# The low parts of the mixers' weights, made in quarters in every slot instead of halves in two slots of four

## The chip, the core and the metric

The program runs on one core of one Trainium2 chip. The core has a matrix engine (TensorE, PE in the profile), a vector engine (VectorE, DVE), an engine for activation functions (ScalarE, ACT), a general one (GpSimd, POOL) and an engine that here only starts DMA transfers (SyncE, SP). Each runs its own list of instructions in order; they meet at semaphores. SBUF is the on-chip memory with 128 partitions, PSUM the memory that PE writes. The metric is the device time of one execution in microseconds, lower is better.

## The reference, cut to what matters

The program is a first block (rotary attention beside an mLSTM, then a gated feed-forward net), then two layers, each a feed-forward net, a mixer and a second feed-forward net, over 256 tokens of width 1024, all in float32:

```python
for i in range(DEPTH_2):                                   # DEPTH_2 = 2
    h = rmsnorm(x, ffn1_norm[i])
    x = x + 0.5 * swiglu(h, ffn1_w_gate[i], ffn1_w_up[i], ffn1_w_down[i])
    h = rmsnorm(x, mix_norm[i])
    proj = h @ w_in[i]                                     # 1024 x 2560: q_s, k_s, v_s, q_m
    mkv = rmsnorm(mem, mem_norm[i]) @ w_mem_kv[i]          # 1024 x 512
    o_m = memory_attention(q_m, k_m, v_m)
    # layer 0: chunked_rel_attention; layer 1: rotary q and k, diff_attention
    x = x + jnp.concatenate([o_s, o_m], axis=-1) @ w_out[i]   # 1024 x 1024
    ...
```

## The kernel before, in words

**Products in three parts.** Every float32 product is made of three rounded ones: with `a = a_hi + a_lo` and `w = w_hi + w_lo`, PE adds `a_hi·w_hi`, `a_hi·w_lo` and `a_lo·w_hi` (function `three`, L1461 to L1463 in the profile). So each weight has to be split before PE can use it.

**Units.** The weights stream through SBUF in units of 128 partitions x 2048 elements (1 MB). A unit takes four steps: SP fetches it into `raw[:, c % 3]` (L326), ACT copies it, rounded, into `whi[:, c % 3]` and increments `hi_done`, DVE subtracts (`wlo = raw - whi`) and increments `lo_done`, PE uses it and increments `unit_used`. Each of the three buffers exists three times. SP may fetch unit c + 3 only when `lo_done` says that unit c has been split; ACT may write `whi` for unit c + 3 only when PE has used unit c.

**A mixer is 60 slots.** In the two mixers (L = 0 and 1) PE, ACT and DVE each run a Python loop `for h in range(SLOTS)` over slots h = 0 to 59, unrolled. In slots 0 to 47 PE makes a quarter of a unit's products (`dense(h)`: six matmuls of 512 columns), in slots 48 to 59 a quarter of an output unit (`out_part(h)`). So PE begins unit n of the mixer (c = u + n, u = MEMU[L]) in slot 4n, and waits there for its `lo_done`:

```python
if h % 4 == 0:
    pe.wait_ge(lo_done, c + 1)
```

Between these products PE puts the attention: scores of item j in slot S_AT[j] (25, 27, 29, 31, 33, 35, 37, 39, 43, 44, 46 to 51), the turn of its probabilities two slots later, the product with the values three slots later. ACT rounds unit n in slots 4n-8 and 4n-7 (a half in each), and does exponentials and copies. DVE, in each of its slots, does in this order: `heads_rest` (L1355), `head_sum` (L896), in layer 1 `differential_norm` (L1402), `head_scale` (L1374), `y_rest` (L1363), `scores` (L987 and L989, or L1002), in layer 1 the rotation of queries and keys (L957, L962, L965; `rotated`), then the low part of a unit (`lo_half`, L1345), then in layer 1 `combine` (L1016 to L1020), then `group_out` (L1390, L1392). Each engine's list is fixed; an engine may be some slots behind another as long as the semaphores allow.

**The low parts in the mixers.** DVE makes the halves of unit n in its slots 4n-6 and 4n-5, and nothing of this kind in 4n-4 and 4n-3. The unit after the mixer's last one (the first of the next feed-forward net) is split in slots 58 and 59.

After the loop `boundary` adds PE's last sums to the residual rows (`residual`, L939) and prepares the next net's input.

Of the kernel before, what the change touches and what calls it, by code (L numbers as in the profile page):

```python
# [44 lines left out]
FFU = [30, 63, 112, 145, 194]  # L45
# [93 lines left out]
def build(nc, t, out):  # L139
# [7 lines left out]
    with ExitStack() as ctx:  # L147
# [702 lines left out]
        def _(dve):  # L850
# [8 lines left out]
            def lo(u, c0=0):  # L859

                dve.wait_ge(hi_done, u + 1)
                v = slice(c0, UW)
                dve.tensor_tensor(wlo[:, u % 3, v], raw[:, u % 3, v], whi[:, u % 3, v], ALU.subtract)\  # L863
                    .then_inc(lo_done, 1)
# [39 lines left out]
            def turned_gain(T, n, parts):  # L904
                for b in parts:
                    dve.wait_ge(xhi_done, 4 * T + b + 1)
                    bank = TURN_BANKS.get(T, range(4))[b]
                    for c in (2 * b, 2 * b + 1):
                        ins = dve.scalar_tensor_tensor(out=xlo[:, c, :], in0=ps[:, bank, SEQ * (c % 2):SEQ * (c % 2) + SEQ],  # L909
                                                       scalar=gain_col(n, c), in1=xhi[:, c, :],  # L910
                                                       op0=ALU.mult, op1=ALU.subtract)
                    ins.then_inc(xlo_done, 1)

            def boundary(T, n, idx, u_last, f, u, banks=(4, 6)):

                if f is not None:
                    dve.wait_ge(frs_ready, FRS_READY[f])
                scale = [1.0 if f is None else frs[:, r:r + 1] for r in range(RT)]
                residual(idx, u_last, scale[0], 0, banks)
                residual(idx, u_last, scale[1], 1, banks, (0,))  # L920
                turned_gain(T, n, (0, 1))
                residual(idx, u_last, scale[1], 1, banks, (1,))
                turned_gain(T, n, (2, 3))
                lo(u + 1)
                if n == N_F1:
                    dve.wait_ge(tr_ps, 4 * T + 4)
                    for r in range(RT):
                        scaled(N_FIN, res, res, r)
                lo(u + 2)

            def residual(idx, u_last, factor, r, banks=(4, 6), parts=range(2)):

                for h in parts:
                    if (r, h) < (1, 1):
                        dve.wait_ge(acc_ready, 3 * idx + 2 * r + h + 1)
                    else:
                        dve.wait_ge(unit_used, u_last + 1)
                    v = slice(512 * h, 512 * h + 512)
                    dve.scalar_tensor_tensor(out=res[:, r, v], in0=ps[:, banks[r] + h, :], scalar=factor,  # L939
                                             in1=res[:, r, v], op0=ALU.mult, op1=ALU.add).then_inc(res_done, 1)  # L940
# [156 lines left out]
            for r in range(RT):  # L1097
                for h in range(2):
                    v = slice(512 * h, 512 * h + 512)
# [236 lines left out]
            for L in range(2):  # L1336
                ffn(1 + 2 * L, FFU[1 + 2 * L], 2)
                u, e0, i0, base = MEMU[L], E0[L], IT0[L], STREAM0 + 12 * L
                T, n, idx, f = T_M0 + 3 * L, N_M0 + 3 * L, R_F1 + 3 * L, 1 + 2 * L

                def lo_half(c, part):

                    dve.wait_ge(hi_done, c + 1)
                    v = slice(1024 * part, 1024 * part + 1024)
                    ins = dve.tensor_tensor(wlo[:, c % 3, v], raw[:, c % 3, v], whi[:, c % 3, v], ALU.subtract)  # L1345
                    if part:
                        ins.then_inc(lo_done, 1)

                def heads_rest(h):
# [32 lines left out]
                def group_out(g):  # L1382

                    i, c = i0 + 4 * g, 16 + 8 * (g % 2)
                    heads, size = (2, 2 * HD) if ITEMS[i][0] == "D" else (4, HD)
                    total = sums[:, 2 * i:2 * i + 8]
                    if heads == 2:
                        total = total.rearrange("p (j e) -> p j e", e=2)[:, :, 0]
                    dve.wait_ge(p_ready, SOFT[i + 3])
                    link(dve.reciprocal(rec[:, c:c + 2 * heads], total))  # L1390
                    dve.wait_ge(pv_ready, i + 4)
                    dve.tensor_tensor(xn[:, :, 256 * g:256 * g + 256].rearrange("p r (h d) -> p r h d", d=size),  # L1392
                                      ps[:, 1, :].rearrange("p (r h d) -> p r h d", r=RT, d=size),
                                      rec[:, c:c + 2 * heads].rearrange("p (r h) -> p r h", r=RT).unsqueeze(3)
                                      .to_broadcast([P, RT, heads, size]), ALU.mult).then_inc(o_copied, 1)
# [19 lines left out]
                for h in range(SLOTS):  # L1415
                    if h in (4, 8):
                        turned_gain(T, n, (h // 2 - 2, h // 2 - 1))
                    if L == 0 and h == S_AT[0]:
                        dve.wait_ge(toep_ready, 1)
                    if h - 1 in HEAD_TURNS:  # L1420
                        heads_rest(h - 1)
                    if 0 <= h - 1 < 40 and (h - 1) % 8 in (5, 7):
                        k = 2 * ((h - 1) // 8) + ((h - 1) % 8 == 7)
                        head_sum(e0 + tile_event(L, k), MH if k // 2 in (0, 2) else 8, HD)
                    if L == 1:
                        for g in (0, 2, 3):
                            if h == V_AT[4 * g + 3] + 2:
                                head_sum(e0 + SUB_EVENT[g], 4, 2 * HD)
                            if h == V_AT[4 * g + 3] + 3:
                                differential_norm(g)  # L1430
                    for r, d in enumerate((9, 10)):
                        if h >= d and (h - d) % 8 == 0 and (h - d) // 8 in (0, 1, 3, 4):
                            head_scale(2 * ((h - d) // 8) + r)
                    if h - 1 in Y_TURNS[L]:
                        y_rest(Y_TURNS[L][h - 1])
                    if h in S_AT:
                        scores(i0 + S_AT.index(h))
                    if L == 1 and (h - 1) // 8 in (1, 3, 4) and (h - 1) % 8 in (5, 7):
                        rotated(2 * ((h - 1) // 8) + ((h - 1) % 8 == 7))
                    if h >= 2 and (h + 6) % 4 < 2:  # L1440
                        lo_half(u + (h + 6) // 4, (h + 6) % 4)
                    if L == 1 and h in S_AT:
                        combine(i0 + S_AT.index(h))
                    if h in V_AT and V_AT.index(h) % 4 == 3:
                        group_out(V_AT.index(h) // 4)
                boundary(T_F2 + 3 * L, N_F2 + 3 * L, R_WO1 + 3 * L, WO[1 + L] + 3, None, FFU[2 + 2 * L])
                if L == 0:
                    ffn(2, FFU[2], 2)
# [562 lines left out]
```

## Time and profile before

| | |
|---|---|
| median of 3 runs | 1406.43 us |
| lowest and highest | 1405.89 and 1407.33 us |
| the profiled execution, its own time | 1406.34 us |
| its span, first to last instruction | 1404.5 us |
| around the span | 1.84 us |
| first mixer, from its first low part in slots to its end | 585.5 to 711.0 us of the span |
| second mixer, the same stretch | 1082.5 to 1208.5 us of the span |
| granted clock of TensorE | 1.00 in the mixers (0.998 over the span) |

The profile is of one execution. Times in a row are microseconds from the start of the span. An instruction's duration overlaps with its follower's by a little (on DVE) or by much (matmuls on PE: 0.39 us long, one started every 0.23 us), so what a row costs its engine is read from the distance of two starts.

### The profile page before, as it was taken

Reading aid. Unit: us, or ns where it says so; the run is one execution under the profiler, and the core shown is the slowest. Engines: PE = TensorE matmul, PEld = TensorE weight load, DVE = VectorE, ACT = ScalarE, POOL = GpSimd, SP = SyncE. Lnnn points to the kernel's source line nnn. Section 1 sums busy time; section 2 is a strip of 40 time slices with the busy share of each in tenths; the row PEclk is TensorE's granted clock in tenths of the full one; section 3 lists DMA queues with packets and bytes.
Section 4 is the critical chain, followed back from the end, with each engine's and each line's share of the span. In section 5 each row is a group of like instructions: output and inputs, shape, how many; then the busy total and the mean of one; then the engine's idle time right before and its main releaser. Section 6 shows DMA issues by size and latency. Waiting matters only on the chain.

```text
span 1404.5 us, 19169 instructions
## 1 busy us (share of the span) xinstructions
PE 1375.3 (98%) x7393; PEld 1166.7 (83%) x7393; DVE 939.6 (67%) x1158; ACT 710.5 (51%) x921; POOL 128.1 (9%) x145
## 2 busy tenths in 40 slices
PE   6999999999999999999999999999999989999998
PEld 5888888888888888888888888888888867788887
DVE  4975676766677666765567666666667778666665
ACT  4656436444464444576654444544445666554442
POOL 3000003000030000032020000100000321300000
PEclk9999999999999999999999999999999999999999
DMA  9444456756546555553355565465665442466561
GB/s 269 155 156 145 150 180 243 236 188 199 181 143 215 183 192 194 164 189 109 109 173 187 181 195 192 135 224 181 192 196 180 155 146 91 143 196 200 181 198 70
DMA packets 165451, 246.33 MB, mean 175 GB/s; under 512 B 5800, under 2 KB 122708, under 8 KB 165264
## 3 DMA queue, kind: packets, MB, share of 16 engines
q1 hardware_dynamic: 161952, 240.14, 52.8%
q0 software_dynamic: 1776, 4.74, 1.2%
q8 instruction: 38, 0.62, 0.2%
q10 hardware_dynamic: 1664, 0.66, 0.2%
q14 instruction: 21, 0.17, 0.0%
HBM read 244.45 MB, written 1.07 MB: 175 GB/s over the span
## 4 chain that ended last, share of the span: by engine, by line
PE 90%; DVE 5%; ACT 2%; DMA 1%; issue 1%; POOL 1%; SPq 0%; ACTq 0%; POOLq 0%; DVEq 0%
PE ps L1509 28%; PE ps L1461 14%; PE ps L1514 14%; PE ps L1463 14%; PE ps L1462 14%; PE ps L1750 2%; PE ps L1721 1%; DMA raw<-in_w_in 1%; ACT xx L559 1%; PE ps L1502 1%; DVE xx L909 1%; DVE wlo L1345 1%; PE ps L1938 0%; DMA res<-in_x 0%; ACT pr L588 0%
## 5 line engine op out<-in xcount | busy, mean ns | idle before, releaser
L1509 PE MATMUL ps<-xx,whi 128*128 128x512 f32 x1760 | 443.5, 393 | 2.8 <-DVE xx L909 2.8
L1509 PEld LDWEIGHTS ps<-xx,whi 128*128 128x128 f32 x1760 | 318.4, 189 | 64.6 <-issue 3.6
L868 DVE TENSOR_TENSOR wlo<-raw,whi 128x2048 fp32r<-128x2048 f32 x120 | 275.1, 2293 | 94.1 <-ACT whi L532 94.1
L532 ACT ACTIVATE whi<-raw 128x2048 fp32r<-128x2048 f32 x120 | 229.5, 1913 | 122.4 <-PE ps L1463 122.4
L524 ACT ACTIVATE whi<-raw 128x2048 fp32r<-128x2048 f32 (+1 forms) x136 | 207.0, 1537 | 99.6 <-PE ps L1463 88.3
L1514 PEld LDWEIGHTS ps<-xx,wlo 128*128 128x128 f32 x1760 | 241.3, 190 | 18.2
L1514 PE MATMUL ps<-xx,wlo 128*128 128x256 f32 x1760 | 246.8, 282 | 0.0
L1461 PE MATMUL ps<-whi,hhi 128*128 128x512 f32 x504 | 199.2, 395 | 1.7 <-DVE hlo L1054 1.7
L1462 PE MATMUL ps<-wlo,hhi 128*128 128x512 f32 x504 | 196.8, 390 | 0.0
L1463 PE MATMUL ps<-whi,hlo 128*128 128x512 f32 x504 | 196.4, 390 | 0.0
L863 DVE TENSOR_TENSOR wlo<-raw,whi 128x2048 fp32r<-128x2048 f32 x76 | 173.4, 2288 | 33.5 <-ACT whi L524 33.4
L1461 PE MATMUL ps<-whi,xx 128*128 128x512 f32 x400 | 163.8, 410 | 1.3 <-DVE xx L909 0.8
L1463 PE MATMUL ps<-whi,xx 128*128 128x512 f32 x400 | 157.3, 393 | 0.0
L1462 PE MATMUL ps<-wlo,xx 128*128 128x512 f32 x400 | 156.6, 392 | 0.0
L618 ACT ACTIVATE sc<-ps 128x512 f32<-128x512 f32 x55 | 32.8, 596 | 163.8 <-PE ps L1514 163.8
L1461 PEld LDWEIGHTS ps<-whi,hhi 128*128 128x128 f32 x504 | 94.9, 188 | 20.4 <-DVE hlo L1054 3.0
L1463 PEld LDWEIGHTS ps<-whi,hlo 128*128 128x128 f32 x504 | 94.6, 188 | 20.3
L1462 PEld LDWEIGHTS ps<-wlo,hhi 128*128 128x128 f32 x504 | 94.9, 188 | 16.9
L424 POOL TENSOR_SCALAR ms<-ss 128x1 f32<-128x1 f32 x18 | 27.1, 1506 | 793.5 <-ACT xn L542 793.3
L624 ACT ACTIVATE pr<-ps 128x512 f32<-128x512 f32 x55 | 32.8, 596 | 131.9 <-PE ps L1514 131.9
L1029 DVE TENSOR_TENSOR sc<-ps,sc 128x512 f32<-128x512 f32 x55 | 38.0, 691 | 90.5 <-ACT sc L618 90.5
L1463 PEld LDWEIGHTS ps<-whi,xx 128*128 128x128 f32 x400 | 75.5, 189 | 16.8
(245 smaller groups left out, 1351.6 us busy)
## 6 DMA issues: line engine op xcount, KB each, us to landing
raw<-in_ffn_w_gate SPq DMA_DIRECT2D x44, 1024.0 KB, 5.3
raw<-in_ffn_w_up SPq DMA_DIRECT2D x44, 1024.0 KB, 5.3
raw<-in_ffn_w_down SPq DMA_DIRECT2D x44, 1024.0 KB, 5.0
raw<-in_w_in SPq DMA_DIRECT2D x41, 1024.0 KB, 5.1
raw<-in_w_gate_up SPq DMA_DIRECT2D x22, 1024.0 KB, 5.1
raw<-in_w_out SPq DMA_DIRECT2D x12, 1024.0 KB, 5.0
raw<-in_w_down SPq DMA_DIRECT2D x11, 1024.0 KB, 5.0
raw<-in_w_mem_kv SPq DMA_DIRECT2D x4, 1024.0 KB, 5.2
```

Source lines behind the costliest of these rows:

```text
L524: ins = act.activation(whi[:, slot, v], raw[:, slot, v], ACT.Copy)
L532: act.activation(whi[:, c % 3, :], raw[:, c % 3, :], ACT.Copy).then_inc(hi_done, 1)
L618: act.activation(halves(gsc), gate_parts(bank)[1], ACT.Copy).then_inc(gate_cross, 1)
L624: act.activation(halves(ups), gate_parts(2)[1], ACT.Copy).then_inc(up_cross, 1)
L863: dve.tensor_tensor(wlo[:, u % 3, v], raw[:, u % 3, v], whi[:, u % 3, v], ALU.subtract)\
L868: dve.tensor_tensor(wlo[:, c % 3, :], raw[:, c % 3, :], whi[:, c % 3, :], ALU.subtract)\
L1029: dve.tensor_tensor(halves(gsc), gate_parts(bank)[0], halves(gsc), ALU.add).then_inc(gate_sum, 1)
L1461: pe.matmul(o, stat[0], mov[0], start=start, stop=False)
L1462: pe.matmul(o, stat[0], mov[1], start=False, stop=False)
L1463: return pe.matmul(o, stat[1], mov[0], start=False, stop=stop)
L1509: return pe.matmul(ps[:, bank + n, :], whi[:, slot, 256 * k + P * n:256 * k + P * n + P], both, start=start, stop=False)
L1514: return pe.matmul(ps[:, bank + n, 0:SEQ], wlo[:, slot, 256 * k + P * n:256 * k + P * n + P], xhi[:, k, :], start=False, stop=stop)
```

## The change

`lo_half` becomes `lo_quarter`: it subtracts 512 of the 2048 elements instead of 1024, and the unit is reported in `lo_done` with its fourth part. DVE makes the parts of unit n in its slots 4n-6, 4n-5, 4n-4 and 4n-3, one in each, at the place in the slot at which the halves stood. The unit after the mixer would be left half done by slot 59, so its last two quarters follow the loop, ahead of `boundary`. There are 15 units with 4 quarters in each mixer, 120 instructions in place of 60. No other engine's list is changed.

```diff
-                def lo_half(c, part):
+                def lo_quarter(c, part):
 
                     dve.wait_ge(hi_done, c + 1)
-                    v = slice(1024 * part, 1024 * part + 1024)
+                    v = slice(512 * part, 512 * part + 512)
                     ins = dve.tensor_tensor(wlo[:, c % 3, v], raw[:, c % 3, v], whi[:, c % 3, v], ALU.subtract)
-                    if part:
+                    if part == 3:
                         ins.then_inc(lo_done, 1)
...
-                    if h >= 2 and (h + 6) % 4 < 2:
-                        lo_half(u + (h + 6) // 4, (h + 6) % 4)
+                    if h >= 2:
+                        lo_quarter(u + (h + 6) // 4, (h + 6) % 4)
...
+                for part in (2, 3):
+                    lo_quarter(FFU[2 + 2 * L], part)
                 boundary(T_F2 + 3 * L, N_F2 + 3 * L, R_WO1 + 3 * L, WO[1 + L] + 3, None, FFU[2 + 2 * L])
```

DVE's list in slots 8 to 11 of either mixer before (L909 fills `xx`, the input of the dense products; L896 is `head_sum`; L1374 is `head_scale`; the last row belongs to slot 14):

```order
L909 SCALAR_TENSOR_TENSOR xx<-ps,gcol,xx 128x256 x4
L896 TENSOR_REDUCE hss<-sq 128x4
L1374 TENSOR_TENSOR work<-work,hrs 128x256 x2
L1345 TENSOR_TENSOR wlo<-raw,whi 128x1024 x2
L896 TENSOR_REDUCE hss<-sq 128x8
```

and in the change:

```order
L909 SCALAR_TENSOR_TENSOR xx<-ps,gcol,xx 128x256 x4
L896 TENSOR_REDUCE hss<-sq 128x4
L1345 TENSOR_TENSOR wlo<-raw,whi 128x512
L1374 TENSOR_TENSOR work<-work,hrs 128x256
L1345 TENSOR_TENSOR wlo<-raw,whi 128x512
L1374 TENSOR_TENSOR work<-work,hrs 128x256
L1345 TENSOR_TENSOR wlo<-raw,whi 128x512 x4
```

The third and fourth quarter of unit 3 (used by PE from slot 12) now stand behind the `head_sum` of slot 8 and the first `head_scale` of slot 9; the halves of this unit stood ahead of all the rows shown.

DVE's list in slots 14 to 18 of the second mixer before (L957 to L965 is the rotation of one tile, L1355 is `heads_rest`), from the low part of slot 14 on:

```order
L1345 TENSOR_TENSOR wlo<-raw,whi 128x1024 x2
L896 TENSOR_REDUCE hss<-sq 128x8
L957 TENSOR_TENSOR work<-work,ropes 128x512
L962 TENSOR_TENSOR work<-work,ropes 128x256 x2
L965 TENSOR_TENSOR work<-work 128x512
L1355 SCALAR_TENSOR_TENSOR heads_t<-ps,colg,heads_t 128x512
L1374 TENSOR_TENSOR work<-work,hrs 128x512 x2
```

and in the change:

```order
L1345 TENSOR_TENSOR wlo<-raw,whi 128x512 x2
L896 TENSOR_REDUCE hss<-sq 128x8
L957 TENSOR_TENSOR work<-work,ropes 128x512
L962 TENSOR_TENSOR work<-work,ropes 128x256 x2
L965 TENSOR_TENSOR work<-work 128x512
L1345 TENSOR_TENSOR wlo<-raw,whi 128x512
L1355 SCALAR_TENSOR_TENSOR heads_t<-ps,colg,heads_t 128x512
L1374 TENSOR_TENSOR work<-work,hrs 128x512
L1345 TENSOR_TENSOR wlo<-raw,whi 128x512
L1374 TENSOR_TENSOR work<-work,hrs 128x512
```

Unit 5, used by PE from slot 20, was complete with the first row; now its last quarter stands behind a `head_sum`, a rotation, a `heads_rest` and a `head_scale`.

DVE's list in slots 32 to 34 of the second mixer before (L987 and L989 are the `scores` of slot 33):

```order
L896 TENSOR_REDUCE hss<-sq 128x8
L957 TENSOR_TENSOR work<-work,ropes 128x512
L962 TENSOR_TENSOR work<-work,ropes 128x256 x2
L965 TENSOR_TENSOR work<-work 128x512
L1374 TENSOR_TENSOR work<-work,hrs 128x512
L987 TENSOR_REDUCE nmax<-ps 128x2
L989 TENSOR_TENSOR nmax<-nmax,small 128x2
L1374 TENSOR_TENSOR work<-work,hrs 128x512
L1345 TENSOR_TENSOR wlo<-raw,whi 128x1024
```

and in the change:

```order
L896 TENSOR_REDUCE hss<-sq 128x8
L957 TENSOR_TENSOR work<-work,ropes 128x512
L962 TENSOR_TENSOR work<-work,ropes 128x256 x2
L965 TENSOR_TENSOR work<-work 128x512
L1345 TENSOR_TENSOR wlo<-raw,whi 128x512
L1374 TENSOR_TENSOR work<-work,hrs 128x512
L987 TENSOR_REDUCE nmax<-ps 128x2
L989 TENSOR_TENSOR nmax<-nmax,small 128x2
L1345 TENSOR_TENSOR wlo<-raw,whi 128x512
L1374 TENSOR_TENSOR work<-work,hrs 128x512
L1345 TENSOR_TENSOR wlo<-raw,whi 128x512
```

A quarter now stands ahead of the scores of slot 33, and another between them and the `head_scale` of slot 34.

## Rows read from the trace of the kernel before

**Rows 1.** The page's head and its part 1.

```profile
span 1404.5 us, 19169 instructions
PE 1375.3 (98%) x7393; PEld 1166.7 (83%) x7393; DVE 939.6 (67%) x1158; ACT 710.5 (51%) x921; POOL 128.1 (9%) x145
```

**Rows 2.** Busy time by stretch, both mixers: from:to, length, then each engine.

```profile
585.50:711.00 125.50, 125.50 (x711) 102.18 (x710) 78.90 (x147) 80.56 (x163) 26.67 (x24) 1.00 0.41 135
1082.50:1208.50 126.00, 118.75 (x648) 94.50 (x647) 100.57 (x212) 80.53 (x166) 28.52 (x30) 1.00 0.41 134
```

**Rows 3.** Waits of PE, 1082 to 1222 us: total, times, longest.

```profile
PE ps L1461 <- ACT pr L588: 1.7, 1, 1.7
...
PE ps L1721 <- DVE work L1020: 1.4, 1, 1.4
PE ps L1461 <- DVE nmax L1002: 1.2, 2, 1.0
PE ps L1955 <- DVE xn L1402: 0.8, 1, 0.8
```

**Rows 4.** Line L1345, whole span: shortest, median and longest duration in ns.

```profile
L1345 DVE TENSOR_TENSOR wlo<-raw,whi x60: 1212/1219/1227, 594.4 to 1208.4; 128x1024 fp32r<-128x1024 f32 x60
```

**Rows 5.** Timeline of DVE: start, duration, instruction; slot 9, first and second mixer.

```profile
607.42 0.42 DVE L1374 TENSOR_TENSOR work<-work,hrs 128x256 f32<-128x256 f32 x1
...
1104.41 0.41 DVE L1374 TENSOR_TENSOR work<-work,hrs 128x256 f32<-128x256 f32 x1
```

**Rows 6.** Timeline of PE: first matmul of slot 12, first and second mixer.

```profile
608.94 0.39 PE L1461 MATMUL ps<-whi,xx 128*128 128x512 f32 x1
...
1105.93 0.39 PE L1461 MATMUL ps<-whi,xx 128*128 128x512 f32 x1
```

**Rows 7.** Timeline of DVE, slot 55 of the second mixer.

```profile
1200.59 0.75 DVE L1363 SCALAR_TENSOR_TENSOR xx<-ps,colg,xx 128x512 fp32r<-128x512 f32 x1
```

**Rows 8.** Timeline of PE, slot 56 of the second mixer, which waited for it.

```profile
1201.48 0.47 PE L1461 MATMUL ps<-whi,xx 128*128 128x512 f32 x1 [0.27 <-DVE xx L1363]
1201.79 0.40 PE L1462 MATMUL ps<-wlo,xx 128*128 128x512 f32 x1
```

**Rows 9.** Timeline of DVE, slots 14 to 18 of the second mixer.

```profile
1109.57 0.69 DVE L896 TENSOR_REDUCE hss<-sq 128x8 f32<-128x512 f32 x1 [0.79 <-ACT sq L578]
1110.18 0.68 DVE L957 TENSOR_TENSOR work<-work,ropes 128x512 f32<-128x512 f32 x1
...
1112.29 2.36 DVE L1345 TENSOR_TENSOR wlo<-raw,whi 128x1024 fp32r<-128x1024 f32 x2
1114.57 0.68 DVE L896 TENSOR_REDUCE hss<-sq 128x8 f32<-128x512 f32 x1
...
1117.29 0.75 DVE L1355 SCALAR_TENSOR_TENSOR heads_t<-ps,colg,heads_t 128x512 fp32r<-128x512 f32 x1
1117.95 1.28 DVE L1374 TENSOR_TENSOR work<-work,hrs 128x512 f32<-128x512 f32 x2
```

**Rows 10.** Timeline of PE: first matmul of slot 20, second mixer.

```profile
1117.30 0.39 PE L1461 MATMUL ps<-whi,xx 128*128 128x512 f32 x1
```

**Rows 11.** Timeline of DVE, second mixer: the half of slot 30, the scores of slot 33.

```profile
1141.12 1.23 DVE L1345 TENSOR_TENSOR wlo<-raw,whi 128x1024 fp32r<-128x1024 f32 x1
...
1148.38 0.68 DVE L987 TENSOR_REDUCE nmax<-ps 128x2 f32<-128x512 f32 x1
```

**Rows 12.** Timeline of PE, second mixer: scores of slot 35, `turn_product` of slot 43.

```profile
1150.55 0.39 PE L1461 MATMUL ps<-heads_t 64*128 64x256 f32 x2 [1.70 <-ACT pr L588]
...
1171.42 0.66 PE L1955 MATMUL ps<-cst,xn 128*128 128x128 f32 x4 [0.19 <-DVE xn L1392]
```

**Rows 13.** Timeline of DVE, slot 56 of the second mixer.

```profile
1202.39 0.68 DVE L896 TENSOR_REDUCE hss<-sq 128x4 f32<-128x512 f32 x1
```

**Rows 14.** Line L326, the fetches of units, 1080 to 1130 us.

```profile
DMA to landing us min/median/max: 5.0/5.1/5.6
```

**Rows 15.** Timeline of ACT: first half of unit 6, slot 16 of the first mixer.

```profile
615.73 1.06 ACT L524 ACTIVATE whi<-raw 128x1024 fp32r<-128x1024 f32 x1
```

## The prediction, before the change was run

> **What bounds the kernel now.** I read the page's head first: PE is busy for 98% of the span [rows 1]. Then the busy time by stretch: in the first mixer PE is busy in all of its 125.5 us, in the second in 118.75 of 126.0 us, while DVE, which the change touches, is busy for 78.9 and 100.6 us [rows 2]. So a mixer's time is PE's list plus what PE stands still, and DVE costs time only where PE waits for it. The list of PE's waits names these places, all in the second mixer: 1.7 us for ScalarE's exponentials of slot 34, 1.4 us for a `combine`, 1.2 us for scores, 0.8 us for `differential_norm` [rows 3]. The first three belong together: on the timeline DVE works without a pause from its slot 30 to slot 34, about two slots behind PE. That gives two questions: does the new order bring DVE sooner to what PE waits for, and does a unit's low part, now reported two slots later, come too late for PE, which does not wait for it anywhere now.
>
> **The price of a quarter.** A half takes 1219 ns [rows 4], but the next instruction starts 1.14 us after it (two halves at 1112.29, the next row at 1114.57, [rows 9]). For 512 elements the trace has no subtraction of a weight, but `head_sum` over 512 elements takes 0.69 us, and its follower starts 0.61 us later [rows 9]. I take 0.60 us from start to start and 0.69 us to the end that a waiter sees. The lowest value would be half of a half, 0.57; the highest is the whole duration, 0.69. A unit costs 2.40 us of DVE instead of 2.28, over 30 units 3.6 us more, of no weight by itself, for DVE idles 25 us or more in each mixer. What counts is order: against before, a slot 4n-6 or 4n-5 gets 0.54 us shorter, a slot 4n-4 or 4n-3 0.60 us longer.
>
> [...]
>
> **Where the report comes late.** The last quarter of unit n stands in DVE's slot 4n-3, PE asks in slot 4n.
> - *Slot 12, both mixers.* Unit 3's halves stood in slots 6 and 7; its last two quarters now stand in 8 and 9. In the first mixer the quarter of slot 8 starts where the first `head_scale` did, at 607.42 [rows 5]; 0.60 later that `head_scale` (duration 0.42, so 0.34 to the next start), then the quarter of slot 9 from 608.36 to 609.05. PE's first matmul of slot 12 is at 608.94 [rows 6]. How PE starts after a wait: DVE's L1363 ended at 1201.34 [rows 7], the matmul came at 1201.48, 0.14 later, and the next one 0.31 after it instead of 0.23 [rows 8]. So 609.05 + 0.14 + 0.08 - 608.94 = 0.33 us. In the second mixer it is 1104.41 + 1.63 + 0.22 against 1105.93 [rows 5, 6]: 0.33 us again.
> - *Slot 20, second mixer.* Here the DVE list between `head_sum` of slot 14 and the last quarter of unit 5 holds two rotations. `head_sum` waits for ScalarE and through it for PE, so it starts at 1109.57 + 0.33 = 1109.90 [rows 9]. Then, from start to start: `head_sum` 0.61, rotation 2.11 (1110.18 to 1112.29), two quarters 1.20, `head_sum` 0.60, rotation 2.11, quarter 0.60, `heads_rest` 0.66, `head_scale` 0.60, last quarter 0.69 to its end: 9.18 us, thus 1119.08. PE wants to begin slot 20 at 1117.30 [rows 10]. 1119.08 + 0.22 - 1117.30 = 2.00 us, of which 0.33 is the shift from slot 12: 1.67 us more. In the first mixer the rotations are missing, 4.22 us less DVE work, so unit 5 is in time there.
> - *All others.* Slots 8, 16 and 24 have the quarters back to back with no more than a `head_sum` between; from slot 28 on PE takes about 2 us a slot, and DVE is idle or at most two slots behind. I count nothing.
>
> **Where DVE was already late (second mixer).**
> - *Slots 30 to 35.* The half of slot 30 [rows 11] becomes a quarter: scores of slot 31 0.54 us earlier. In slot 31 half or quarter lies under ScalarE's exponentials, for which `combine` waits either way. PE's waits for scores and `combine` shrink by 0.54. But slot 32 gets a quarter ahead of the scores of slot 33 (now 1148.38, [rows 11]), whose exponentials PE awaits in slot 35 [rows 12]: +0.60. What PE won by waiting less in slot 33 it waits more in slot 35. Sum +0.06 us.
> - *Slot 43.* Halves in 38 and 39 -1.08, quarters in 40 and 41 +1.20, half in 42 -0.54: DVE reaches `group_out` 0.42 us sooner. PE waits only 0.19 for it [rows 12]: -0.19 us.
> - *Slots 56 and 57.* From slot 53 on +0.60, -0.54, -0.54: the `head_sum` of slot 56 [rows 13] starts 0.48 us sooner, and through GpSimd so does `differential_norm`, for which PE waits 0.8 [rows 3]: -0.48 us. The new quarter of slot 56 lies under DVE's wait for GpSimd.
> - *The end.* Four quarters, 2.40 us, in place of two halves, 2.28, ahead of `residual`; DVE waits there for PE for longer than the difference. Nothing.
>
> **The sum.** 0.33 + 0.33 + 1.67 + 0.06 - 0.19 - 0.48 = +1.72 us. The profiled execution took 1406.34 us (span 1404.5 and 1.84 around it), so 1408.06; the median lies 0.09 above it: **1408.1 us**. With a quarter at 0.57 the chains are 0.03 us shorter per quarter: about 1407.9.
>
> **Fetches.** SP may refill `raw` only after the report, so unit 6 of the first mixer is fetched at 609.1. It lands 5.1 us later [rows 14], at 614.2, or at 614.7 with the longest, and ScalarE takes it at 615.73 [rows 15]. Hidden, with 1.0 us to spare; PE's own shift of 0.33 widens it.
>
> **Rivals.**
> 1. *A quarter costs DVE its whole duration, 0.69 us.* Each quarter in a chain adds 0.09: one at each slot 12, three more in the slot 20 chain, a half turned into a quarter saves 0.45 instead of 0.54: slots 30 to 35 cost 0.24, the gain at 43 vanishes and that at 57 falls to 0.21. 0.42 + 0.42 + 1.94 + 0.24 - 0.21 = 2.8, so 1409.2. [...] For it: the durations. Against: all neighbours on the timeline start 0.08 to 0.09 before their forerunner's end. Chance 0.15.
> 2. *PE meets no late unit*: DVE gets through slots 8 to 17 sooner than my chains, for instance because ScalarE's squares come earlier once DVE delays nothing. Then only +0.06 - 0.19 - 0.48 stays: 1405.8. Against it: in slot 20 DVE would have to be 2 us faster. Chance 0.10.
> 3. *The even spread dissolves DVE's backlog in slots 30 to 35*, and PE's 1.7 + 1.4 + 1.0 us [rows 3] go: 1406.43 + 1.72 - 0.06 - 4.1 = 1404.0, or below 1402.5 with rival 2. Against it: between the scores of 31 and of 33 there is one quarter more, not less. Chance 0.04, and it is the way to faster.
> 4. *Later fetches collide.* Units 6 and 7 are now asked for within 3 us (609.1 and, with four quarters after the second `head_scale`, about 612); if each holds up the other by half a transfer time, 2.5 us, unit 6 lands at 616.7 to 617.2, 1.0 to 1.5 us after ScalarE wants it, say 1.2, and PE follows in both mixers: 1408.1 + 2.4 = 1410.5. It decides from a landing of 6.6 us on; the longest is 5.6 [rows 14]. Chance 0.05, slower.
>
> **How the numbers follow.** My own case has a chance of 0.66, with 1407.2 to 1408.9 for it. About 0.2% (2.8 us) is what a measurement of this kernel can tell from no change, so slower begins at 1409.25 and faster ends at 1403.6. Slower: rival 4 (0.05), a bit under half of rival 1 (0.06), and 0.05 for a chain that I counted too short (a unit late in another slot): 0.16. Faster: 0.04. Same: 0.80, though the likeliest sign is plus. The range 1405.7 to 1409.5 leaves out rivals 3 and 4 and the tails.
>
> **What would show each step.** In the profile after: 120 subtractions of 128x512, starts 0.60 apart in a row; a wait of PE for line L1345 (none now), three times: about 0.2 us in slot 12 of each mixer and 1.6 us in slot 20 of the second. PE's wait for the exponentials in slot 35 grows from 1.7 to about 2.3 us, those for scores and `combine` shrink by 0.5 together, the wait for `differential_norm` falls to 0.3. The first mixer stays as long within 0.4 us, the second becomes about 1.4 us longer. I am wrong if no wait of PE for L1345 shows, if it shows in further slots, or if ScalarE waits for a fetch.

## The result, and the profile after

| | before | after |
|---|---|---|
| median | 1406.28 us (22 runs, 1405.09 to 1407.41) | 1408.70 us (22 runs, 1407.08 to 1411.33) |
| profiled execution | 1406.34 us, span 1404.5 | 1408.64 us, span 1406.8 |

The ratio is 1.0020, with a 95% interval of 1.0013 to 1.0026: the change makes the kernel 2.4 us slower, the interval is +1.8 to +3.7 us. The forecast was 1408.1 us, in a range of 1405.7 to 1409.5.

Head of the page, and busy time by stretch (both mixers), of the changed kernel:

```profile
span 1406.8 us, 19231 instructions
PE 1377.7 (98%) x7393; PEld 1168.1 (83%) x7393; DVE 943.6 (67%) x1218; ACT 710.4 (50%) x921; POOL 126.9 (9%) x145
```

```profile
585.50:711.00 125.50, 125.50 (x710) 101.83 (x709) 80.89 (x176) 80.33 (x162) 24.10 (x24) 1.00 0.40 135
1082.50:1208.50 126.00, 117.23 (x638) 92.62 (x637) 100.70 (x237) 80.21 (x166) 30.12 (x30) 1.00 0.37 126
```

Against [rows 1, 2] DVE has 60 instructions more, and in the 126 us of the second mixer PE is busy for 1.5 us less. The places are in the waits of PE from 1080 us on, and in the line of the low parts (its 120 instructions, and who waited for it):

```profile
PE ps L1463 <- ACT pr L588: 2.3, 1, 2.3
...
PE ps L1463 <- DVE wlo L1345: 1.5, 1, 1.5
PE ps L1723 <- DVE work L1020: 1.4, 1, 1.4
PE ps L1463 <- DVE nmax L1002: 0.7, 2, 0.4
PE ps L1463 <- DVE xx L1363: 0.6, 1, 0.6
PE ps L1957 <- DVE xn L1402: 0.6, 1, 0.6
```

```profile
L1345 DVE TENSOR_TENSOR wlo<-raw,whi x120: 679/684/694, 594.2 to 1211.4; 128x512 fp32r<-128x512 f32 x120
...
  PEld ps L1463: 2.8, 3
  PE ps L1463: 1.5, 1
```

PE's lines stand two lower than before (L1463 was L1461). New against [rows 3] is the wait of 1.5 us for a low part; the three waits of the weight loads show where units come late: slot 12 of both mixers and slot 20 of the second (PE itself stands still for only 0.15 us in slot 12, too little for this list). The wait for the exponentials grew by the 0.6 us that was worked out, that for scores shrank by 0.5. The wait for `differential_norm` shrank by 0.2 only, where 0.5 was expected, and the one for `xx` ahead of it (slot 56) grew from 0.3 to 0.6, of which the prediction has nothing.

**Slot 12.** PE in the first mixer, changed kernel:

```profile
608.06 0.39 PE L1463 MATMUL ps<-whi,xx 128*128 128x512 f32 x1
...
608.89 0.50 PE L1463 MATMUL ps<-whi,xx 128*128 128x512 f32 x1
609.23 0.40 PE L1464 MATMUL ps<-wlo,xx 128*128 128x512 f32 x1
...
615.87 0.60 PE L1940 MATMUL ps<-cst,work 128*128 128x128 f32 x4
```

The first of these rows, in slot 11, was at 608.26 before, the last one at 615.74: this execution is 0.20 us ahead of the other up to slot 12 and 0.13 behind it after. Slot 12 starts at 608.89, 0.38 after its forerunner instead of 0.23, and its second matmul 0.34 after the first. The late unit costs 0.33 us. In the second mixer the same count gives 0.28 us.

**Slot 20 of the second mixer.** DVE from slot 9 to slot 18, and PE's start of slot 20:

```profile
1104.55 0.68 DVE L1345 TENSOR_TENSOR wlo<-raw,whi 128x512 fp32r<-128x512 f32 x1
1105.15 0.42 DVE L1374 TENSOR_TENSOR work<-work,hrs 128x256 f32<-128x256 f32 x1
1105.48 0.69 DVE L1345 TENSOR_TENSOR wlo<-raw,whi 128x512 fp32r<-128x512 f32 x1
1107.42 0.42 DVE L1374 TENSOR_TENSOR work<-work,hrs 128x256 f32<-128x256 f32 x1 [1.26 <-POOL hrs L436]
1107.77 2.49 DVE L1345 TENSOR_TENSOR wlo<-raw,whi 128x512 fp32r<-128x512 f32 x4
1110.18 0.68 DVE L896 TENSOR_REDUCE hss<-sq 128x8 f32<-128x512 f32 x1
...
1117.41 0.75 DVE L1355 SCALAR_TENSOR_TENSOR heads_t<-ps,colg,heads_t 128x512 fp32r<-128x512 f32 x1
1118.07 0.68 DVE L1374 TENSOR_TENSOR work<-work,hrs 128x512 f32<-128x512 f32 x1
1118.67 0.69 DVE L1345 TENSOR_TENSOR wlo<-raw,whi 128x512 fp32r<-128x512 f32 x1
```

```profile
1119.41 0.50 PE L1463 MATMUL ps<-whi,xx 128*128 128x512 f32 x1 [1.52 <-DVE wlo L1345]
```

From the start of the `head_sum` of slot 14 to the end of the last quarter of unit 5 it is 1119.36 - 1110.18 = 9.18 us, the sum of the prediction to the hundredth. PE's products with `cst` two slots on (L1938 before, L1940 now) came at 1120.03 before and at 1122.27 here, 2.24 us later. With the start offset of -0.20 and the two slots 12, slot 20 cost 2.24 + 0.20 - 0.33 - 0.28 = 1.83 us, where 1.67 was predicted. The rest is the start of the chain, 0.15 us later than predicted: `head_sum` no longer waits for ScalarE (0.79 us of idle time ahead of it in [rows 9], none now) but for DVE itself, which had stood still for 1.26 us ahead of a `head_scale`, for GpSimd. GpSimd's first operation there, `hms` at 1104.72, took 1.50 us. In the profiles of two later kernels with the same list at this place (the two runs that move only unit 15's last quarters, below) it took 0.56, `head_sum` waited for ScalarE as predicted, and slot 20 cost 1.70 and 1.67 us. So the 0.16 us do not belong to every execution; what decides between 0.56 and 1.50 stays open.

**Slots 52 to 57, second mixer.** GpSimd turns the sums of `head_sum` into factors in two small operations, `hms` and `hrs` (L433 and L436), and `differential_norm` (L1402) waits for them. DVE and GpSimd in the changed kernel:

```profile
1198.54 0.68 DVE L1345 TENSOR_TENSOR wlo<-raw,whi 128x512 fp32r<-128x512 f32 x1
1200.40 0.69 DVE L1402 TENSOR_TENSOR xn<-xn,hrs 128x512 f32<-128x512 f32 x1 [1.18 <-POOL hrs L436]
...
1206.75 0.69 DVE L1402 TENSOR_TENSOR xn<-xn,hrs 128x512 f32<-128x512 f32 x1 [1.18 <-POOL hrs L436]
```

```profile
1198.71 0.57 POOL L433 TENSOR_SCALAR hms<-hss 128x4 f32<-128x4 f32 x1 [29.57 <-DVE hss L896]
1199.36 1.01 POOL L436 TENSOR_TENSOR hrs<-hms,mhalf 128x4 f32<-128x4 f32 x1
1205.06 0.57 POOL L433 TENSOR_SCALAR hms<-hss 128x4 f32<-128x4 f32 x1 [4.68 <-DVE hss L896]
```

and the same operation before, where no subtraction stood behind `head_sum` in these slots:

```profile
1196.64 0.20 POOL L433 TENSOR_SCALAR hms<-hss 128x4 f32<-128x4 f32 x1 [28.80 <-DVE hss L896]
1203.15 0.20 POOL L433 TENSOR_SCALAR hms<-hss 128x4 f32<-128x4 f32 x1 [5.22 <-DVE hss L896]
```

`hms` takes 0.57 us instead of 0.20 and ends 0.06 us after the subtraction beside it (1199.28 and 1199.22). From `head_sum` (1197.94 and 1204.29) to `differential_norm` it is 2.46 us, twice, instead of 2.09 and 2.08 (from 1195.87 and 1202.39 before): the change puts a quarter just where DVE had been idle, and the idle time was not free. From one `differential_norm` to the next `head_sum` it is 3.89 us instead of 4.43. So these slots cost 0.37 + 0.37 - 0.54 = 0.20 us where the prediction had a gain of 0.48.

**The sum** as the trace shows it, with the predicted terms in brackets: slots 12 0.33 and 0.28 (0.33 and 0.33), slot 20 1.83 (1.67), slots 30 to 35 0.06 (0.06), slot 43 -0.22 (-0.19), slots 52 to 57 +0.20 (-0.48): 2.48 us (1.72). Less the 0.20 us by which this execution was ahead when it came to the mixers, that is the 2.3 us between the two spans.

### The profile page after: what moved, and what is told of

It is laid out like the page before. It is cut to its first block, busy times and chain, and to the rows that moved or that the text cites. A ratio compares the mean times of both kernels' runs of the same rounds, so it can differ in the third digit from the quotient of the medians.

```text
span 1406.8 us, 19231 instructions
## 1 busy us (share of the span) xinstructions
PE 1377.7 (98%) x7393; PEld 1168.1 (83%) x7393; DVE 943.6 (67%) x1218; ACT 710.4 (50%) x921; POOL 126.9 (9%) x145
## 4 chain that ended last, share of the span: by engine, by line
PE 91%; DVE 4%; ACT 2%; POOL 1%; issue 1%; DMA 0%; SPq 0%; ACTq 0%; DVEq 0%; POOLq 0%
PE ps L1511 28%; PE ps L1463 15%; PE ps L1516 14%; PE ps L1465 14%; PE ps L1464 14%; PE ps L1752 2%; PE ps L1723 1%; PE ps L1504 1%; DVE xx L909 1%; ACT xx L559 1%; ACT pr L588 0%; PE ps L1940 0%; DVE wlo L1345 0%; DMA res<-in_x 0%; POOL hrs L436 0%
## 5 line engine op out<-in xcount | busy, mean ns | idle before, releaser
L1463 PE MATMUL ps<-whi,hhi 128*128 128x512 f32 x504 | 199.2, 395 | 1.7 <-DVE hlo L1054 1.7
L1463 PE MATMUL ps<-whi,xx 128*128 128x512 f32 x400 | 165.1, 413 | 2.9 <-DVE wlo L1345 1.5
L1463 PEld LDWEIGHTS ps<-whi,hhi 128*128 128x128 f32 x504 | 94.9, 188 | 20.5 <-DVE hlo L1054 3.0
L1463 PEld LDWEIGHTS ps<-whi,xx 128*128 128x128 f32 x400 | 76.3, 191 | 18.4 <-DVE wlo L1345 2.8
```

Source lines behind the costliest of these rows:

```text
L1463: pe.matmul(o, stat[0], mov[0], start=start, stop=False)
```

## The experiments

In all of these kernels `lo_quarter` is replaced by a function that takes any part of a unit, and a table says in which slots of a mixer the parts stand:

```diff
-                def lo_half(c, part):
+                def low(c, a, b):
 
                     dve.wait_ge(hi_done, c + 1)
-                    v = slice(1024 * part, 1024 * part + 1024)
+                    v = slice(a, b)
...
-                    if h >= 2 and (h + 6) % 4 < 2:
-                        lo_half(u + (h + 6) // 4, (h + 6) % 4)
+                    for m, a, b in LOW[L].get(h, ()):
+                        low(u + m, a, b)
```

Without an entry in `MOVED`, halves stand in slots 4n-6 and 4n-5 and quarters in 4n-6 to 4n-3. Each kernel was run 11 times (one of them 6 times) beside the kernel before, whose median was 1406.34, 1406.36 and 1406.25 us on the three occasions. Lines of these kernels are higher by 16 (DVE, ACT, POOL) or 18 (PE). In the first four (those of the next section) the low parts of the mixers' input, made in slots 4 and 8, are scaled with a wrong column of gains, so what these four compute is not the right result. The instructions are the same and take the same time (the four of a slot 1.66 us in their traces and in the others), and the first kernel of the section on GpSimd has the right column and the late units in halves as well.

The intervals reach about 1.3 us to either side, so a time alone cannot tell terms of a few tenths. For these the traces are compared: from PE's scores of slot 25 to the first `residual`, about the last two thirds of the second mixer, it is 83.51 us in the kernel before and 83.54 in the changed one. This stretch lies behind slots 12 and 20 and leaves them out.

### Where the time goes: one mixer at a time, and the late units

```diff
+QUARTERS = (all units, none)        # first mixer alone
+QUARTERS = (none, all units)        # second mixer alone
+QUARTERS = (all but 3, all but 3 and 5)
```

First mixer alone. 

> Quarters in the first mixer alone, halves as before in the second. My theory (PE waits for a low part that is reported too late): the first mixer has one late unit, unit 3 at slot 12, 0.33 us, and nothing else of weight: +0.3 us against before. Rival (what costs is the work itself, 60 more instructions and 0.06 us more of DVE time for each, wherever they stand): half of the whole change's +2.4 us, so +1.2 us.

Measured 1406.54 us, ratio 1.0001 (0.9992 to 1.0010), 0.2 us more than before. The interval still holds the rival's +1.2; the next three runs decide against it. One wait of the weight loads for a low part, 0.4 us long, as in slot 12 of the changed kernel.

Second mixer alone. 

> Quarters in the second mixer alone, halves as before in the first. My theory: slot 12 0.3, slot 20 1.8, slots 30 to 35 +0.06, slot 43 -0.2, slots 52 to 57 +0.2 (as the profile of the whole change has them): +2.1 us against before, and a wait of PE for L1345 of 1.5 us. Rival (the amount of work): +1.2 us.

Measured 1409.51 us, ratio 1.0021 (1.0012 to 1.0030): +3.2 us, the whole of the change's loss and 1.1 us above the expected 2.1. The four of its 11 runs with a mean clock of 0.998 or more have a median of 1408.05 us, +1.7; the others are a matter of the last section. PE waits 1.5 us for a low part and 2.3 us for the exponentials.

Quarters, but the late units in halves. 

> The whole change, but for three of the 30 units: unit 3 of both mixers and unit 5 of the second are made in halves in slots 4n-6 and 4n-5, as before. My theory: these three hold all of the loss by late reports, 0.33 + 0.28 + 1.82 = 2.4 us; what stays is +0.06 - 0.22 + 0.20, so +0.0 to +0.1 us against before, with no wait of PE for L1345. Rival (the amount of work, 54 of 60 more instructions remain): +2.1 us.

Measured 1406.33 us, ratio 1.0003 (0.9994 to 1.0012). No wait for a low part is left, and with three units of thirty in halves the loss is gone. 54 of the 60 added subtractions are still there, and the rival's +2.1 lies outside the interval: their number is not what costs. The stretch from slot 25 to `residual` is 83.54 us, +0.03, where +0.06 - 0.22 + 0.20 was expected.

The late report without quarters: before, with the second half of unit 5 in slot 17 instead of 15.

```diff
+MOVED = {(1, 5): ((14, 0, 1024), (17, 1024, 2048))}
```

> The kernel before, with one instruction moved: the second half of unit 5 of the second mixer from slot 15 to slot 17 (behind head_sum, rotation, heads_rest and head_scale). The work is the same. My theory: from head_sum of slot 14 at 1109.57 us: 0.61 + 2.11 + 1.14 + 0.60 + 2.11 + 0.66 + 0.60 + 1.22 to the end of this half = 1118.62; + 0.22 - 1117.30 = 1.5 us that PE waits in slot 20; +1.5 us against before. Rival (the amount of work, or the later fetches of all units): 0.

Measured 1407.79 us, ratio 1.0010 (1.0001 to 1.0019), with this wait in the second mixer:

```profile
PE ps L1479 <- DVE wlo L1361: 1.2, 1, 1.2
```

The same loss at the same place, out of halves. So it is the place of a unit's last part that costs, and not the size of the parts.

### GpSimd beside a subtraction

The changed kernel without units 3 and 5 in quarters, and with unit 14 in halves and unit 15 in slots 54, 55, 57 and 57, so that no subtraction follows a `head_sum` in slots 52 and 56:

```diff
+QUARTERS = (all but 3, all but 3, 5, 14 and 15)
+MOVED = {(1, 15): ((54, 0, 512), (55, 512, 1024), (57, 1024, 1536), (57, 1536, 2048))}
```

> Units 3 (both mixers) and 5 (second) in halves as in the run before, and in the second mixer also unit 14 in halves in slots 50 and 51, and unit 15 in quarters in slots 54, 55, 57 and 57: no subtraction stands any more between a head_sum and the differential_norm that waits for GpSimd (slots 52, 53, 56). My theory (a DVE subtraction beside GpSimd's two small instructions holds these up): from the start of head_sum to differential_norm 2.08 us as before, not 2.46 as in the changed kernel; sum +0.06 - 0.22 - 0.53 = -0.7 us against before. Rival (GpSimd's own scatter): 2.46 stays and the sum is about -0.2 us.

Measured 1405.53 us, ratio 0.9994 (0.9984 to 1.0003), 0.8 us under the kernel with unit 5 and 3 in halves alone. The interval reaches 1, but the stretch from slot 25 to `residual` shows the gain: 82.84 us, 0.70 less than in that kernel. No wait for a low part is there either. GpSimd's two `hms` take 0.20 us again, PE waits 0.2 us for `differential_norm`.

The kernel before with unit 15's halves in slots 56 and 57 instead of 54 and 55:

```diff
+MOVED = {(1, 15): ((56, 0, 1024), (57, 1024, 2048))}
```

> The kernel before, with the two halves of unit 15 of the second mixer moved from slots 54 and 55 to 56 and 57, off the chain from differential_norm (slot 53) through group_out (54) and head_sum (56) to differential_norm (57). head_sum of slot 56 then starts at 1201.26, right after y_rest, instead of 1202.39, and PE's wait of 0.76 us goes: -0.75 us against before. The half of slot 56 now runs beside GpSimd's work. If DVE holds GpSimd up: 2.4 to 2.5 us from head_sum to differential_norm; if the longer time in the changed kernel was scatter: 2.08. Rival for the time (PE is the bound all along and its wait only moves): 0.

Measured 1405.08 us, ratio 0.9993 (0.9984 to 1.0002). The size of the delay was wrong: from `head_sum` to `differential_norm` it is not 2.4 to 2.5 but 2.99 us (1201.69 to 1204.68), and PE's wait for it is 0.5 us and not gone. The stretch from slot 25 to `residual` is 83.32 us, only 0.19 less than before, so the lower median is not explained by the move and its interval reaches 1. GpSimd's first operation ends 0.05 us after the half (1202.29, 1.22 us long) does:

```profile
1202.46 1.10 POOL L449 TENSOR_SCALAR hms<-hss 128x4 f32<-128x4 f32 x1 [4.11 <-DVE hss L912]
```

So the delay is no fixed price but lasts as long as the subtraction. The trace of the kernel before has the same picture, ahead of any change: in slots 6 to 7 of the second mixer the first of two halves (1.22 us long, so to 1100.65) stands behind `head_sum`, and `hms` ends 0.05 us after it. It also has GpSimd beside a DVE instruction with one of its two inputs in PSUM (`residual`):

```profile
1099.43 2.35 DVE L1345 TENSOR_TENSOR wlo<-raw,whi 128x1024 fp32r<-128x1024 f32 x2
1212.76 0.69 DVE L939 SCALAR_TENSOR_TENSOR res<-ps,res 128x512 f32<-128x512 f32 x1 [0.67 <-PE ps L1463]
```

```profile
1099.60 1.10 POOL L433 TENSOR_SCALAR hms<-hss 128x4 f32<-128x4 f32 x1 [7.86 <-DVE hss L896]
1212.94 0.29 POOL L424 TENSOR_SCALAR ms<-ss 128x1 f32<-128x1 f32 x1 [8.50 <-ACT xn L542]
```

`ms`, a like operation, takes 0.29 us here, 0.29 us too at 399.75, where DVE is idle, and 1.51 us at 1089.60, beside a 2048-wide `wlo<-raw,whi`. So it is not any DVE instruction that holds GpSimd up. Two runs on the changed kernel put the length of the delay to the test; the only edit is where the third and fourth quarter of unit 15 stand.

```diff
+MOVED = {(1, 15): ((54, 0, 512), (55, 512, 1024), (57, 1024, 1536), (57, 1536, 2048))}
```

> The changed kernel, but the third quarter of unit 15 of the second mixer is made in slot 57, beside the fourth, and no longer in slot 56 behind head_sum. My theory (GpSimd cannot read its operand while a subtraction with two SBUF operands runs on DVE): the distance from the head_sum of slot 56 to the differential_norm of slot 57 falls from 2.46 to 2.08 us, GpSimd's first operation from 0.57 to 0.20, PE's wait for differential_norm from 0.6 to 0.2, the time by 0.37 us against the changed kernel, to about 1408.3. The distance one slot pair earlier (slot 53, whose quarter is untouched) stays 2.46. Rival (GpSimd's times vary by themselves): both distances stay 2.46, the time 1408.7.

The time is 1409.57 us (ratio 1.0022, 1.0013 to 1.0031), which tells nothing about 0.4 us. The trace does:

```profile
1198.58 0.57 POOL L449 TENSOR_SCALAR hms<-hss 128x4 f32<-128x4 f32 x1 [29.58 <-DVE hss L912]
...
1204.92 0.20 POOL L449 TENSOR_SCALAR hms<-hss 128x4 f32<-128x4 f32 x1 [4.68 <-DVE hss L912]
```

The operation whose neighbour was moved takes 0.20 us, the other, whose neighbour stayed, 0.57, in one execution. The distances to `differential_norm` are 2.10 (moved) and 2.46 us, PE's wait for it is 0.2 us, and from PE's scores of slot 25 to the first `residual` it is 83.19 us instead of 83.54: -0.35 for -0.37. So the delay comes with the subtraction beside it; that GpSimd cannot read its operand meanwhile was the author's idea of the cause, and no run shows it.

```diff
+MOVED = {(1, 15): ((54, 0, 512), (55, 512, 1024), (56, 1024, 1536), (56, 1536, 2048))}
```

> The changed kernel, but the third and the fourth quarter of unit 15 of the second mixer both stand in slot 56, behind head_sum. My theory (GpSimd is blocked until the last of the subtractions ends, and finishes 0.05 us after it): two quarters end 1.88 us after head_sum's start, so GpSimd's first operation takes about 1.2 us, differential_norm follows 3.05 us after head_sum's start, PE waits 1.2 us for it instead of 0.6, the time is 1409.3. Rival (meeting a subtraction costs GpSimd a fixed 0.37 us, or it gets its operand between two subtractions): 2.46 us, a wait of 0.6, 1408.7.

```profile
1203.15 1.28 DVE L1361 TENSOR_TENSOR wlo<-raw,whi 128x512 fp32r<-128x512 f32 x2
1205.33 0.69 DVE L1418 TENSOR_TENSOR xn<-xn,hrs 128x512 f32<-128x512 f32 x1 [0.90 <-POOL hrs L452]
```

```profile
1203.32 0.57 POOL L449 TENSOR_SCALAR hms<-hss 128x4 f32<-128x4 f32 x1 [4.68 <-DVE hss L912]
1203.97 1.32 POOL L452 TENSOR_TENSOR hrs<-hms,mhalf 128x4 f32<-128x4 f32 x1
```

Neither theory held. `hms` waited for the first quarter only (0.57 us, as with one); then `hrs` met the second one and took 1.32 instead of 1.01 us. The distance is 2.78 us, between 2.46 and 3.05, and PE's wait 0.9 us. In this run GpSimd was held up operation by operation, for 0.37 and for 0.31 us. From slot 25 to `residual` it is 83.87 us, 0.33 more than in the changed kernel. 1410.23 us (6 runs; ratio 1.0028, 1.0016 to 1.0041).

### What PE waits for besides

The kernel before with unit 9's halves in slots 31 and 33 instead of 30 and 31:

```diff
+MOVED = {(1, 9): ((31, 0, 1024), (33, 1024, 2048))}
```

> The kernel before, with the halves of unit 9 of the second mixer moved from slots 30 and 31 to 31 and 33. The half of slot 31 lies under ScalarE's exponentials; that of slot 33 stands behind the scores for which PE waits. DVE reaches the scores of slots 31 and 33 1.14 us sooner. PE's waits for scores (1.0), combine (1.4) and exponentials (1.7) shrink from 4.1 to 2.9: -1.1 us against before. Rival (the stall is ScalarE's, DVE only fills it): 0. If the clock is lowered during the wait, as in the profiles of the runs before, the gain is partly hidden and smaller.

Measured 1406.25 us, ratio 1.0001 (0.9992 to 1.0010): the expectation failed. The scores of slot 35 did come 1.1 us sooner (1149.11, in an execution 0.3 us ahead, against 1150.55 in [rows 12]), but the stretch to `residual` is 83.51 us as before, since one slot on stands a wait that the kernel before does not have:

```profile
1152.70 1.10 PE L1768 MATMUL ps<-work,pT 128*128 128x64 f32 x8 [0.99 <-ACT pT L617]
```

ScalarE copies `pT` for it at 1152.07, behind a square that waits for DVE's `group_out` of slot 34:

```profile
1151.54 0.63 ACT L844 ACTIVATE sq<-xn 128x512 f32<-128x512 f32 x1 [2.48 <-DVE xn L1408]
1152.07 0.58 ACT L617 ACTIVATE pT<-ps 128x512 f32<-128x512 f32 x1
```

and `group_out` stands behind the halves of slots 33 and 34. The same edit together with unit 12 in slots 43 and 44 and unit 15 in 56 and 57:

> Three moves of halves in the second mixer, no quarters: unit 9 to slots 31 and 33, unit 12 from 42 and 43 to 43 and 44, unit 15 to 56 and 57. -1.14, -0.19 and -0.75 add up if each removes its own wait of PE: -2.1 us against before, 1404.3. Rival (the places are not independent, what is won is waited for at the next): -1.1 us or less.

Measured 1405.70 us, ratio 0.9997 (0.9988 to 1.0006), 0.7 us under the kernel before (the stretch 0.52 shorter) instead of 2.1: the rival's case, with the same new wait of 1.0 us. The last two runs take it away, by moving unit 10's halves from 34 and 35 to 35 and 36, behind `group_out`; the second has unit 15 in quarters besides, none of them in slot 56.

```diff
+MOVED = {(1, 9): ((31, 0, 1024), (33, 1024, 2048)),
+         (1, 10): ((35, 0, 1024), (36, 1024, 2048)),
+         (1, 15): ((54, 0, 512), (55, 512, 1024), (57, 1024, 1536), (57, 1536, 2048))}   # second run only
```

> The kernel before, but in the second mixer unit 9's halves stand in slots 31 and 33 (as in the earlier run on unit 9) and unit 10's in 35 and 36 instead of 34 and 35. Expected: group_out of slot 34 comes 1.14 us sooner too, so ScalarE's square and the copy of pT behind it do, and PE's new wait of 1.0 us for pT in slot 36 goes; PE's waits for scores and combine shrink as they did. The time is 1.1 us under the kernel before, about 1405.3, with no wait for the low parts of unit 10. Rival: the 1.1 us is given back again at a later wait (the rotations of slots 37 and 38, slot 43), and the time is that of the kernel before, 1406.4.

> The same as the run on units 9 and 10, and unit 15 of the second mixer in quarters in slots 54, 55, 57 and 57 (nothing in slot 56). Expected: -1.1 us as there and -0.7 more, since head_sum of slot 56 starts earlier with GpSimd's first operation still 0.20 us, together about 1404.6. Rival: only the second part is left, 1405.7.

PE's waits in the second of them, 1080 to 1215 us:

```profile
PE ps L1479 <- ACT pr L604: 1.7, 1, 1.7
...
PE ps L1739 <- DVE work L1036: 1.3, 1, 1.3
...
PE ps L1973 <- DVE xn L1418: 0.2, 1, 0.2
```

No wait for `pT` is left. From the scores of slot 25 to the first `residual` it is 83.51 us in the kernel before, 82.35 in the first of these (-1.16, for -1.1) and 81.84 in the second (-1.67, for -1.8). The times are 1406.06 us (0.9999, 0.9989 to 1.0008) and 1404.80 us (0.9992, 0.9983 to 1.0001). The second is the lowest of all, 1.45 us under the kernel before, but its interval still reaches 1: that it beats the kernel before is likely and not shown. Why the first one's median lies only 0.2 us lower when its stretch is 1.2 us shorter may have to do with the clock (last section). Its profiled execution is the fastest of its 11 (1403.92 us), but it was 1.3 us ahead already at slot 25, which the stretch does not count.

## Why the prediction was right, and where a term was not

- **The bound** (PE's list plus what PE stands still, DVE only through its order): right. 54 extra subtractions at other places cost nothing that shows. The prediction's list of PE's waits leaves out the second longest, 1.6 us for the `group_out` of slot 50 (L1392); it came to no harm, being 1.5 us after the change.
- **A quarter costs 0.60 us from start to start, 0.69 to its end**: right. The chain of slot 20 took 9.18 us, four quarters in a row 2.41. Rival 1 (0.69 each) came to nearly the measured time, 1409.2 for 1408.7, for a reason that is not there: it would have made the chain 9.45 us long.
- **PE's start after a wait** (0.14 us to the first matmul, 0.08 more behind it): right in its sum, by luck. The first matmul came 0.05 and 0.06 us after the quarter, and what followed cost 0.13 and 0.18 us, since not only the second matmul was late: 0.18 and 0.24 for 0.22.
- **Slots 12 and 20**: three late units, where they were expected, and no fourth. That they are the loss is shown by taking them away (1406.33 us) and by making one of them out of halves (+1.4 us). Rival 2 falls. Slot 20 was 0.16 us dearer in this profile, since a `head_scale` waited for GpSimd beforehand: `hms` took 1.50 us where it took 0.30 before, and ended 0.05 us after a row of quarter, `head_scale` and quarter. In the first mixer it met the same row and took 0.56, ending 0.05 us after the first quarter, and so it did in the second mixer of the two kernels named above. That quarters hold `hms` up is seen each time; why once for the whole row was not tested.
- **Slots 30 to 35, and 43**: +0.06 and -0.22 for +0.06 and -0.19. Rival 3 falls: the waits for the exponentials, `combine` and scores are 2.3, 1.4 and 0.7 us.
- **Slots 56 and 57: the step that failed.** "The new quarter of slot 56 lies under DVE's wait for GpSimd" took DVE's idle time for a cover. GpSimd's operation is held up beside the subtraction, so DVE's own way from `head_sum` to `differential_norm` grew by 0.37 us. It did so in slot 53 too, where the prediction takes the quarter of slot 52 for covered without a word. The rows at 1099.43 and 1099.60 of the trace before could have told. The term is +0.20 and not -0.48, 0.68 us off, which is nearly all of the difference between the sums 1.72 and 2.48.
- **Fetches** (rival 4): hidden. ScalarE waits for none in the mixers; their fetches land within 4.8 to 6.2 us in the first and 4.7 to 5.9 in the second, under the 6.6 us from which the rival would count.

GpSimd's `hms` took 0.20 us beside an idle DVE, 0.57 beside a 512-wide subtraction, 1.10 beside a 1024-wide one, and ended 0.05 or 0.06 us after it. The subtraction reads `raw` and `whi`, both in SBUF. Other DVE instructions in the trace before, ahead of any change, give the same picture: beside a 512-wide product of the rotation (1115.17, 0.68 us long), whose inputs `work` and `ropes` lie in SBUF too, `hms` took 0.57 us, while beside `residual`, one input of which is in PSUM, `ms` took the 0.29 us that it takes beside an idle DVE. The prediction should have weighed these rows; with 0.37 us twice its last gain becomes a small loss (-0.48 + 0.74 = +0.26). The other way round no delay showed: in the changed kernel a quarter at 1143.36 began while `hrs` ran (1142.07 to 1143.75) and took 0.69 us as ever, and all 120 took 679 to 694 ns.

## What to carry to other kernels

Splitting an operation finer costs next to nothing here (0.06 us of DVE for each cut, on an engine that has the time); what costs is that its last part, the one that others wait for, moves later. Before such a change, write down for each consumer when the last part ends and when it is asked for; three places of thirty made the whole loss. And an engine's idle time is a free place only if the engine it waits for is not slowed by what is put there, as GpSimd was here by a subtraction of two SBUF operands (0.57 us for 0.20 in `hms`): look at who works in the gap, and look in the trace before the change for a place where the two already meet. When a wait is cut, look one slot on for the next one that depends on the same engine's list.

## What was not expected of the hardware

One more thing showed in the granted clock. In 6 of the 14 profiles the granted clock of TensorE fell from 1.00 to 0.50 for about 3 us, in or after the second mixer's waits of slots 31 to 35. In the run with quarters in the second mixer alone it was 0.50 from 1153 to 1156 us, just after PE's wait of 2.29 us, and PE then made its matmuls at 0.43 us from start to start instead of 0.23. PE's rows there, and its clock (the 1.00 to 0.80 column) by stretch:

```profile
1152.58 0.39 PE L1479 MATMUL ps<-heads_t 64*128 64x256 f32 x2 [2.29 <-ACT pr L604]
...
1154.53 0.63 PE L1480 MATMUL ps<-wlo,xx 128*128 128x512 f32 x1
1154.96 0.63 PE L1481 MATMUL ps<-whi,xx 128*128 128x512 f32 x1
...
1159.32 0.39 PE L1479 MATMUL ps<-heads_t 64*128 64x256 f32 x2
```

```profile
1145.00:1150.00 5.00, 3.62 (x22) 2.82 (x19) 4.31 (x11) 2.75 (x7) 2.25 (x2) 1.00 0.00 0
1150.00:1155.00 5.00, 2.71 (x15) 2.04 (x14) 4.90 (x11) 2.27 (x7) 0.00 (x0) 0.80 0.40 113
```

From the scores of slot 35 to those of slot 37 it is 6.74 us here, and 5.40 in the profile of the changed kernel (1152.85 to 1158.25), where the clock is 1.00: 1.34 us more. Where the fall lay ahead of such a wait it cost nothing, since PE waited less instead: in the run with quarters in the first mixer alone, whose second mixer is that of the kernel before, the clock is 0.69 from 1145 to 1150 us, PE's wait for the exponentials is 0.35 us instead of 1.70, and from slot 25 to `residual` it is 83.49 us for 83.51.

This bears on the size of the result. Of the 22 runs of the changed kernel 12 had a mean clock of 0.997 or more and a median of 1408.3 us (1407.1 to 1408.7), and 10 had 0.996 and 1409.9 us (1409.6 to 1411.3). The kernel before has both clocks without such a gap (in one series 1406.3 us at 0.996, 5 runs, and 1406.3 at 0.998, 19 runs). So about 2.0 us of the 2.4 is the order of work that this document explains. The rest may come with the longer wait of PE in slot 35, behind which the lower clock falls on work. That is seen in the one profile above and was not tested, and a mean clock of 0.996 does not prove such a fall: the profile of the run with unit 5's half in slot 17 has 0.996 as well, its fall in the mixer (0.66 from 1145 to 1150 us) lies ahead of the wait, and its stretch of 83.53 us has lost nothing. The kernel with units 9 and 10 moved has a like spread, 1404.8 us at 0.999 (4 runs) and 1407.8 at 0.996 (2 runs), which may be why its median hides its gain.
